# Order of dimensions in shifted-copy reads, zero pads in the u tiles, and transposes between weight loads in a gated-conv/Conformer layer on eight cores

## What is computed

```
mod = silu(c) @ w_ada + b_ada                  # shift, scale, gate
h   = rmsnorm(x, norm_g) * (1 + scale) + shift
p   = h @ w_in                                 # a_in a_b a_c a_z | b_v b_g b_z, 7 blocks of 512
y_a = a_b * dwconv3(a_c * a_in) * silu(a_z)
u   = dwconv31(b_v * sigmoid(b_g)) + conv_b_b  # zero padded at both ends of a sequence
y_b = silu(head_layernorm(u)) * silu(b_z)      # 8 groups of 64 channels
y   = x + gate * (concat(y_a, y_b) @ w_out)
out = rmsnorm(y, final_g)
```

## Time and profile before

| | us |
|---|---|
| median of 3 runs | 2893.28 |
| lowest, highest | 2884.27, 3020.43 |
| the profiled execution | 2867.06 |
| its span, slowest core (core 6) | 2865.4 |
| spans of the other cores | 2842.1 to 2864.8 |

### The profile page before, as it was taken

The page is one execution under the profiler, slowest core; times in us unless marked ns, Lnnn a source line. Parts: engine busy times, 40 slices in busy tenths (PEclk is TensorE's granted clock), DMA queues, the critical chain, the costliest instruction groups (busy, mean ns, idle before and its releaser), DMA issues.

```text
span 2865.4 us, 38717 instructions; the slowest of 8 cores (2842.1 to 2865.4 us)
## 1 busy us (share of the span) xinstructions
PE 2299.8 (80%) x11427; PEld 996.9 (35%) x11652; DVE 1139.4 (40%) x1911; ACT 1150.7 (40%) x1922; POOL 550.2 (19%) x574
## 2 busy tenths in 40 slices
PE   2487697979889696987979779895989869798766
PEld 0133243434334243333434334342433324343322
DVE  0124162452616244261635327162452615445136
ACT  1022533526263352525445252633526244353534
POOL 2111411212111121111212141111312132021302
PEclk8798898989999898998999889897999979999888
DMA  9945553543536354363536445364553646355545
GB/s 233 106 90 114 163 166 100 154 122 122 163 108 177 91 171 105 115 166 110 166 109 171 128 144 168 114 177 125 150 156 114 169 131 186 118 139 138 140 122 167
DMA packets 308216, 401.70 MB, mean 140 GB/s; under 512 B 185224, under 2 KB 241712, under 8 KB 299824
## 3 DMA queue, kind: packets, MB, share of 16 engines
q1 hardware_dynamic: 289216, 391.55, 48.8%
q0 software_dynamic: 7392, 7.34, 2.7%
q10 hardware_dynamic: 11408, 0.33, 0.3%
HBM read 254.95 MB, written 84.43 MB: 118 GB/s over the span
## 4 chain that ended last, share of the span: by engine, by line
PE 52%; DMA 27%; SPq 6%; issue 5%; ACT 3%; DVE 3%; ACTq 2%; POOL 1%; another core or an unknown queue 0%; DVEq 0%; POOLq 0%
PE pb L452 35%; PE pb L660 14%; DMA xb<-x 8%; DMA V<-u_scratch 7%; DMA u_scratch<-u 6%; DMA xb<-w_out 5%; PE pb L573 3%; ACTq L290 2%; SPq L563 2%; SPq L343 1%; SPq L433 1%; DMA YP<-gst 1%; DMA yB<-YP 1%; PE pb L587 1%; SPq L356 1%
## 5 line engine op out<-in xcount | busy, mean ns | idle before, releaser
L452 PE MATMUL pb<-hT,w_in_sb 128*128 128x512 bf16 x7008 | 1613.6, 386 | 105.8 <-ACT tp L458 52.6
L452 PEld LDWEIGHTS pb<-hT,w_in_sb 128*128 128x128 bf16 x7168 | 705.7, 99 | 994.8 <-issue 196.7
L573 PE MATMUL pb<-V,WC 128*32 128x512 bf16 x2048 | 176.5, 499 | 334.4 <-DMA V<-u_scratch 268.4
L458 ACT ACTIVATE tp<-pb 128x512 f32<-128x512 f32 x384 | 224.8, 590 | 537.7 <-PE pb L452 438.9
L461 DVE TENSOR_TENSOR t<-pb,tp 128x512 bf16<-128x512 f32 x128 | 88.6, 693 | 732.0 <-PE pb L452 500.1
L619 POOL TENSOR_TENSOR YP<-tp,YP 128x512 bf16<-128x512 f32 x128 | 146.0, 1162 | 675.7 <-ACT tp L617 647.2
L660 PE MATMUL pb<-w_out_sb,yB 128*128 128x512 bf16 x944 | 252.8, 381 | 18.5 <-DMA yB<-YP 13.1
L660 PE MATMUL pb<-w_out_sb,yA 128*128 128x512 bf16 x977 | 252.7, 381 | 2.6 <-ACT tp L458 1.7
L686 ACT ACTIVATE tp<-xb 128x1024 bf16<-128x1024 f32 x125 | 132.0, 1056 | 298.5 <-DVE xb L671 184.3
L314 ACT ACTIVATE tp<-xb 128x1024 bf16<-128x1024 f32 x128 | 134.8, 1054 | 265.0 <-DMA xb<-x 201.6
L671 DVE TENSOR_TENSOR xb<-pb,xb 128x512 f32<-128x512 f32 x250 | 168.1, 687 | 170.0 <-PE pb L660 158.3
(11 more groups left out here) (84 smaller groups left out, 1307.9 us busy)
## 6 DMA issues: line engine op xcount, KB each, us to landing
xb<-x SPq DMA_DIRECT2D x253, 512.0 KB, 7.7
V<-u_scratch SPq DMA_DIRECT2D x128, 527.5 KB
y<-xb SPq DMA_DIRECT2D x125, 512.0 KB, 3.2
xb<-w_out SPq DMA_DIRECT2D x39, 512.0 KB, 23.8
u_scratch<-u SPq DMA_DIRECT2D x128, 128.0 KB, 3.5
YP<-gst SPq DMA_DIRECT2D x64, 256.0 KB, 5.5
yB<-YP SPq DMA_DIRECT2D x120, 128.0 KB, 3.1
w_in_sb<-w_in POOLq DMA_DIRECT2D x14, 512.0 KB, 30.2
```

The lines of the kernel that those rows point to most:

```text
L452: T.op("tensor", lambda e, bank=bank, kc=kc: e.matmul(bank[:], lhsT=w_in_sb[:, kc, col0:col0 + 128], rhs=hT2[q][:, kc, :], start=(kc == 0) ...
L458: T.op("scalar", lambda e: e.activation(out=t[:], in_=bank[:], func=func, scale=scale), reads=[bkey], writes=[tkey])
L573: T.op("tensor", lambda e, s=s, g=g: e.matmul(bank[32 * g:32 * g + 32, :], lhsT=WC[:, (4 * u + g) * 4 + s, :], rhs=vb[:, 4 * hl + g, 4 * s ...
```

## The change

Three things are changed.

1. **V reads.** The source's dimensions go from [4 shifts, 16 channel groups, 4220] to [16 channel groups, 4 shifts, 4220], so the partitions of V are (group, shift) instead of (shift, group). `_wsel` on the host and the sum of the identity in `build_conv_w` (one add, one reduction over groups of four, one scaling) follow that layout.
2. **Pads.** The four u tiles are 528 wide instead of 512 and are cleared once on GpSimd. The product is written to their middle. The u write of a sequence's first or last window takes the zero columns along. `u_pad` and its ten DMAs are gone, and so are the waits for them.
3. **The start.** The transposes of q = 0 are issued between the eighth and the ninth w_ada load; the four x loads of q = 1 follow after the last w_ada load. The first w_in load waits for the 14th w_ada load instead of the 16th.

```
-        UR = Ring("u", [sb("u%d" % i, [128, NT], BF16) for i in range(4)], T)
+        UR = Ring("u", [sb("u%d" % i, [128, VW], BF16) for i in range(4)], T)
...
+        for i in range(4):
+            T.op("gpsimd", lambda e, i=i: e.memset(UR.bufs[i][:], 0.0), writes=[("u", i)])
...
-            for n in (64, 32, 16):
-                T.op("vector", lambda e, n=n: e.tensor_tensor(out=E16[:, 0:n], in0=E16[:, 0:n], in1=E16[:, n:2 * n], op=ALU.add),
-                     reads=["identf"], writes=["identf"])
-            T.op("vector", lambda e: e.tensor_scalar(out=E16[:, 0:16], in0=E16[:, 0:16], scalar1=0.5, scalar2=None, op0=ALU.mult),
+            T.op("vector", lambda e: e.tensor_tensor(out=identf[:, 0:64], in0=identf[:, 0:64], in1=identf[:, 64:128], op=ALU.add),
+                 reads=["identf"], writes=["identf"])
+            T.op("vector", lambda e: e.tensor_reduce(out=identf[:, 64:80], in_=identf[:, 0:64].rearrange("p (c k) -> p c k", k=4),
+                                                     axis=mybir.AxisListType.X, op=ALU.add), reads=["identf"], writes=["identf"])
+            T.op("vector", lambda e: e.tensor_scalar(out=E16[:, 0:16], in0=E16[:, 64:80], scalar1=0.5, scalar2=None, op0=ALU.mult),
...
-        def u_pad(w, side):
-            c = 0 if side == 0 else PAD + NT
-            out = U_d[w].rearrange("a j (p g) t -> (a j p) g t", g=8)[:, :, c:c + PAD]
-            T.dma("scalar", lambda e: e.dma_start(out=out, in_=t1[0][:, 0, 0:8 * PAD].rearrange("p (g t) -> p g t", g=8)),
-                  reads=[("t1", 0, 0)], writes=[("Upad", w, side)], semkey=("up", w, side))
...
-                T.op("vector", lambda e: e.scalar_tensor_tensor(out=ub[:], in0=t[:], scalar=1.0, in1=bank[:], op0=ALU.add, op1=ALU.mult),
+                T.op("vector", lambda e: e.scalar_tensor_tensor(out=ub[:, PAD:PAD + NT], in0=t[:], scalar=1.0, in1=bank[:], op0=ALU.add, op1=ALU.mult),
-                T.dma("sync", lambda e: e.dma_start(out=u_rows(w, q, j, PAD, NT), in_=ub[:]),
+                lo, hi = 0 if wfirst[w] else PAD, VW if wlast[w] else PAD + NT
+                T.dma("sync", lambda e: e.dma_start(out=u_rows(w, q, j, lo, hi - lo), in_=ub[:, lo:hi]),
...
-                deps = [("U", q, j, p), ("Upad", p, 0) if wfirst[p] else ("Uh", q, j, p - 1), ("Upad", p, 1) if wlast[p] else ("Uh", q, j, p + 1)]
+                deps = [("U", q, j, p)] + ([] if wfirst[p] else [("Uh", q, j, p - 1)]) + ([] if wlast[p] else [("Uh", q, j, p + 1)])
-                src = bass.AP(src.tensor, src.offset + par, [[1, 4], [VN, 16], [1, VN - 4]])
+                src = bass.AP(src.tensor, src.offset + par, [[VN, 16], [1, 4], [1, VN - 4]])
...
-            bufs = [mod_load(kc, third, VS, pin=True) for kc, third in order]
+            bufs = [mod_load(kc, third, VS, pin=True) for kc, third in order[:8]]
+            a_half(0, 0)
+            a_half(0, 1)
+            a_transpose(0)
+            bufs += [mod_load(kc, third, VS, pin=True) for kc, third in order[8:]]
+            a_load(0, 1, range(4))
...
-            a_load(0, 1, (0, 1))
-            a_half(0, 0)
-            a_half(0, 1)
-            a_load(0, 1, (2, 3))
-            a_transpose(0)
...
-                load_w(blk, kh, after=[bufs[-1][1]] if (blk, kh) == (5, 0) else [])
+                load_w(blk, kh, after=[bufs[13][1]] if (blk, kh) == (5, 0) else [])
...
-    out = np.empty((2, 4, 16, 32, 4, 2), np.float32)
+    out = np.empty((2, 16, 4, 32, 4, 2), np.float32)
...
-                    out[par, kap, :, :, s, q] = wp[tap if 0 <= tap < KB else KB].reshape(32, 16).T
+                    out[par, :, kap, :, s, q] = wp[tap if 0 <= tap < KB else KB].reshape(32, 16).T
```

More of the change, by code:

```diff
@@ L477, in second_of @@
                 ub, ukey = UR.next()
-                T.op("vector", lambda e: e.scalar_tensor_tensor(out=ub[:], in0=t[:], scalar=1.0, in1=bank[:], op0=ALU.add, op1=ALU.mult),
+                T.op("vector", lambda e: e.scalar_tensor_tensor(out=ub[:, PAD:PAD + NT], in0=t[:], scalar=1.0, in1=bank[:], op0=ALU.add, op1=ALU.mult),
                      reads=[tkey, bkey], writes=[ukey])
-                T.dma("sync", lambda e: e.dma_start(out=u_rows(w, q, j, PAD, NT), in_=ub[:]),
+                lo, hi = 0 if wfirst[w] else PAD, VW if wlast[w] else PAD + NT
+                T.dma("sync", lambda e: e.dma_start(out=u_rows(w, q, j, lo, hi - lo), in_=ub[:, lo:hi]),
                       reads=[ukey], writes=[("U", q, j, w)], semkey=("uw",) + ukey)
-                sides = ([] if wfirst[w] else [(w - 1, PAD + NT, 0)]) + ([] if wlast[w] else [(w + 1, 0, NT - PAD)])
+                sides = ([] if wfirst[w] else [(w - 1, PAD + NT, PAD)]) + ([] if wlast[w] else [(w + 1, 0, NT)])
                 if len(sides) == 2:
@@ L485, in second_of @@
                     dst = bass.AP(dst.tensor, dst.offset, [[VW, 128], [2 * 8 * 128 * VW - PAD - NT, 2], [1, PAD]])
-                    T.dma("sync", lambda e: e.dma_start(out=dst, in_=ub[:].rearrange("p (a t) -> p a t", t=PAD)[:, 0:NT // PAD:NT // PAD - 1, :]),
+                    src = ub[:].rearrange("p (a t) -> p a t", t=PAD)[:, 1:NT // PAD + 1:NT // PAD - 1, :]
+                    T.dma("sync", lambda e: e.dma_start(out=dst, in_=src),
                           reads=[ukey], writes=[("Uh", q, j, w)], semkey=("uh",) + ukey)
@@ L924, in period0 @@
                                        writes=["fg_bc"], semkey="ld_fg"))
-            ends = [(w, 0) for w in range(nwin) if wfirst[w]] + [(w, 1) for w in range(nwin) if wlast[w]]
-            for i, (w, side) in enumerate(ends):
-                add(post, i // 2, lambda w=w, side=side: u_pad(w, side))
             add(post, 11, lambda: t1_halo(0))
```

## The result

The changed kernel takes 0.8257 of the time of the kernel before, with a 95% interval of 0.8088 to 0.8425. Its profiled execution took 2395.8 us for a span of 2394.3 us, and another run 2374.46 us; 2386 was predicted. Executions in which a whole die ran at a lower granted clock are in none of these numbers.

A forecast was written before the change was run, and what follows sets the result against it. TensorE, nearest its limit, waited 268.4 us for V reads running on four DMA engines. First stretch 202, 14 periods of 141 (1974) and last stretch 187 sum to a span of 2363 us, forecast time 2386 us; range 2330 to 2520.

The forecast's parts named there:

- V's term: Middle periods: TensorE's residual wait for the first V pair, 0.5 us a window, bounds 0 and 4.
- those for ScalarE, the w_out windows and the clock (1 + 1.8 + 1.6): Additions per middle period: 1 us leftover ScalarE waits, 1.8 us for reloading w_out, 1.6 us lower clock and gaps.
- The x loads find free queues, and their waits with them: Middle periods: x loads no longer held up, ScalarE's 201.6 us of waits for x falling below 40 us.
- The stall of 52.6 us: Start: TensorE's idle time behind ScalarE's pad writes, 39.16 + 13.46 us, claimed to go with the ten DMAs.
- The charge of 8 us for a new wait: Start, after the pad writes go: w_in comes late next, a new wait of 8 us (0 to 25).
- SyncE will stand until 22.3 us: Start: SyncE stands before the transposes until the fourth scaled tile at 22.3 us, w_ada and x loads behind it.
- w_ada ends about where it does now: Start: 6.3 MB queued before the transposes last past 23 us, so the engines do not run dry.
- the 8 us priced for a failed cover: Start: up to 8 us lost if the queued 6.3 MB did not keep the DMA engines busy during SyncE's stand.
- Rival 4: Whole kernel: TensorE's clock falls to 13/16 under the denser load, time 2893 us, no change; chance 0.06.
- rival 1: Middle periods: ScalarE takes over as the bound, about 150 us a period, span 2513 us; chance 0.18.
- rival 2: V reads: order of dimensions changes nothing, four engines stay, only the start gains, time 2829 us; chance 0.04.
- Rival 3: V reads: 16 engines reading the same memory hinder one another, 25 us a pair giving 3055 us; chance 0.03.

The follow-up runs named there:

- e11_after: The changed kernel once more, unchanged, in a second comparison with five runs; ratio 0.8208 to the kernel before, median 2361.43 us.
- e5: The kernel before with its own partition order, each V read issued as four DMAs of 16 rows, one for each shift; 2485.87 us.
- e6: The changed kernel with each V read issued as two DMAs of 8 channel groups x 4 shifts; 2426.59 us.
- e7: The kernel before with each V read issued as two DMAs of 2 shifts x 16 channel groups; 3364.23 us.
- e10: The changed kernel with each V read issued as four DMAs of 4 channel groups x 4 shifts; 2646.92 us.
- e2: The kernel before with only the zero pads moved into the u tiles and the ten pad writes gone; ratio 0.9851 to the kernel before.
- e3: The kernel before with only the start's new order, transposes of q = 0 between the w_ada loads; ratio 1.0001 to the kernel before.
- e4: The changed kernel with the old order of the start, so V reads and pads only; ratio 0.8259 to the kernel before.

## Why the prediction was right, and where its terms were off

The predicted span was 202 + 1974 + 187 = 2363 us; measured were 207.5 + 1993.2 + 193.6 = 2394.3, and 2358.3 in e11_after. The step from span to run, the factor 1.0097, was too large: it took in that other executions of the kernel before were longer than the profiled one. A run of either kernel takes 1.5 to 1.7 us more than the span of its slowest core, and e11's five runs lie within 12 us of the profiled span. That 2386 lies between the two runs of 2374.46 and 2395.8 is partly luck: the span was forecast 31 us too low for this core, and the factor put 23 back.

**V on all engines: right mechanism, landing time too short.** The share of 1.06 and the return of a landing time confirm the step, and e5, e6, e7 and e10 show that the number outside sets the number of engines. The landing of a V read is 7.5 us by the median, and 6.0 was predicted for a pair. The first pair of a window begins to move 1.9 us after its issue, moves for 5.6 us, and the convolution starts 1.0 us behind its last packet (medians of the trace). The data term was 4.4 us, from 16 x 15 = 244 GB/s. An engine's eight rows of 548 to 610 ns are indeed 4.4 to 4.9 us, so the 15 GB/s an engine of the earlier trace rows held. That it did is luck as far as the runs show: it is not what an engine moves (26 GB/s in e6, e7 and e10), and what slows the rows with 16 engines is open. The 0.6 us between the two issues and other transfers between the rows make up the rest of the 5.6. What the sum had too small is the landing put together from the 3.2 us of y<-xb. TensorE was ready 4.7 us after the issue in the window shown and 7.1 in the median, and 6.5 was counted on. So 28.5 us of waits are left in 14 windows, 2.0 each instead of 0.5. The term lay within its bounds of 0 and 4.

**The period.** 1993.2 / 14 = 142.4 us on the core shown and 138.6 on core 4, which stood at a clock of 0.99; predicted were 141. Of the 142.4, some 2 are the stretch at 0.81 below. In all cores of e11 it is 138.3 to 140.1. So V's term was 1.5 too small, and those for ScalarE, the w_out windows and the clock (1 + 1.8 + 1.6) were too large together by 2 to 4 us. TensorE's leftover waits for ScalarE hardly exist, but not by the path that was given for them. "The x loads find free queues, and their waits with them" failed: x takes 8.0 us to landing, 7.7 before, and ScalarE still waits 179.2 us for it, where below 40 was the sign. Its squares come in time all the same, so in this kernel ScalarE's idle time behind x costs TensorE nothing. Why TensorE's waits for ScalarE went with those for V is not shown.

**The last stretch.** 193.6 us, and 187 were predicted. Its first wait is down to 2.70 us from 11.01, but a transfer hT<-YP makes 6.03 us, and waits of 3.38, 2.35 and 2.18 us stand behind ScalarE and VectorE.

**Pads: right.** The stall of 52.6 us is gone in e2 and in the changed kernel. The charge of 8 us for a new wait was right in size and wrong in place. The first stretch gave 58.8 us instead of 64. Below, the start of the changed kernel: TensorE, then SyncE's queue.

```profile
37.87 4.96 PE L363 MATMUL pb<-V,scT 128*32 128x512 f32 x12 [8.46 <-DMA V<-w_ada]
...
63.83 1.86 PE L449 MATMUL pb<-hT,w_in_sb 128*128 128x512 bf16 x4 [11.50 <-DVE hT L346]
...
156.42 15.70 PE L449 MATMUL pb<-hT,w_in_sb 128*128 128x512 bf16 x72 [1.35 <-DVE tp L411]
177.57 2.40 PE L449 MATMUL pb<-hT,w_in_sb 128*128 128x512 bf16 x5 [5.45 <-DVE hT L346]
```

```profile
14.05 16.89 SPq L340 DMA_TRANSPOSE hT<-xs  x4
...
110.93 30.04 SPq L398 DMA_DIRECT2D tp<-b_gate  x4
141.06 2.15 SPq L303 DMA_DIRECT2D xb<-x  x4
```

The gate's small loads (L398) hold SyncE for 30.04 us, the x loads of window 1 stand behind them until 141.06, and hT of window 1 comes 5.45 us late. Another 1.35 us stand behind VectorE's sum for the gate (L411), which needs those loads. w_in itself made only 0.48 us of wait on this core.

**The new order of the start: wrong.** The steps that failed are "SyncE will stand until 22.3 us" and "w_ada ends about where it does now". The fourth scaled tile is ready at 19.3 us, but four transposes take 16.89 us to issue, until 30.9. The w_ada loads behind them are late and TensorE waits 8.46 us for one. That is the 8 us priced for a failed cover. The projections start at 63.8 us on this core and at 57 to 64 on all, where 59 was predicted, and e3 and e4 show that even this start is worth nothing in the time: the work behind it is bound by w_in and by the queues. Of the predicted 12 us, some 4 reach the first convolution and none can be measured in the time.

**Rival 4, in a weak form.** The stretch from 520 to 670 us of the changed kernel, first on core 0, then on core 4. Only TensorE's busy time and count, the clock, the DMA share and GB/s are shown.

```profile
520.00:670.00 150.00, 149.53 (x641) 0.82 0.52 132
```

```profile
520.00:670.00 150.00, 145.45 (x771) 0.99 0.60 167
```

Cores 0 and 1 stood about 161 us at 0.81 of the clock, a level between 0.50 and 1.00; 161 x (1 - 0.81) = 30 us of the 59 by which core 0 trails cores 2 and 4; the rest is of the size by which the cores differ in e11 too (33 us). It is the 13/16 that the Trainium skill's page "TensorE: Matmul & The Clock Gate" names in "Seeing it yourself" for a whole die, here on two cores of a die and not on all four. The traces of e2, e4, e7 and e10 have such stretches too, up to 319 us a core and always on pairs of neighbouring cores (0 and 1, 2 and 3, 4 and 5, 6 and 7); the other traces, e11's among them, have none. The rest of the program and all of e11 stand at 0.98 to 0.99 by the mean, as predicted, and e7, where TensorE has the longest waits, has the level while e11 does not, so the denser load does not by itself take the clock down. What does is open. ScalarE did not take over (rival 1), and the order of dimensions had its effect (against rival 2). Rival 3 is there in a weak form as well: on 16 engines a V row takes 548 to 610 ns where 319 is the least, but a pair lands in 7.5 us and not in 21.

## What to carry to other kernels

Look at the DMA share while one transfer is alone in flight: 0.12, 0.25 or 0.50 is 2, 4 or 8 engines of 16, and a large issue without a time to landing in the page is the same sign; putting a dimension of 16 outside made 16% here. A rate per engine changes with the number of engines and the layout (26 GB/s in e6, 14 to 15 in the changed kernel), and a landing time added up from that of another transfer came out 1.5 us short, so a margin of 0.5 us is none. An earlier start is worth only what the next queue behind it lets through: list those that it passes (SyncE behind the transposes, w_in, the gate's loads), and take a wait of an engine off the critical path for a consequence until something waits for it.

## What the runs showed of the hardware

- With 2, 4, 8 and 16 outside, a V read shows a DMA share of 0.12, 0.25, 0.50 and 1.06.
- A row of 8,440 bytes took an engine 319 ns (26 GB/s) with 2, 4 or 8 engines in e7, e10 and e6, 554 to 570 in the first two pairs of a window before, 548 to 610 on 16 engines, and 885 to 1017 on 16 engines with the partitions of e5.
- Issuing eight DMAs for a V pair takes SyncE 3.5 to 4.8 us with 16 rows each and 5.5 to 6.0 with 4 rows by 4 shifts; two DMAs take 1.2.
- Four transposes behind queued loads held SyncE's queue for 16.89 us, and four small gate loads for 30.04.
- The granted clock has a level of 0.81, which two neighbouring cores of a die showed for 161 us while the other two did not; in five of the thirteen traces it came, on such pairs, for up to 319 us.
